# Two output products with their first two blocks interleaved, and the branch sum's high part made by ScalarE

## The chip, the cores and the metric

One core of one Trainium2 chip runs the whole program. The metric is the device time of one execution in microseconds (us), of which the median of several runs is given. The engines are TensorE (PE, with its weight loads as PEld), VectorE (DVE), ScalarE (ACT), GpSimd (POOL) and SyncE (SP), which here issues the loads of weights.

## The reference, cut to what matters

The model is a stack of two blocks of layers over 256 tokens of width 1024: an attention and retention mixer, a short convolution mixer, two layers of product-key experts, and then a second block with a feed-forward layer, a token mixer and another feed-forward layer. Two places matter here, the output products of the convolution mixer and of the token mixer:

```python
def short_conv_mixer(xn, w_in, conv_w, w_out):
    bg, cg, hx = jnp.split(xn @ w_in, 3, axis=-1)
    u = cg * hx
    y = lax.conv_general_dilated(u, ...)
    return (bg * y) @ w_out

def token_mixer(h, ..., w_branch_fox, w_branch_swa, w_out):
    ...
    y = jax.nn.sigmoid(ga) * (o_fox @ w_branch_fox) + jax.nn.sigmoid(gb) * (o_swa @ w_branch_swa)
    return y @ w_out
```

All weights and activations are fp32.

## The kernel before

Activations stand transposed: 128 partitions hold 128 of the 1024 features, so that an activation is K = 8 input parts of 128 x 256 tokens. A weight matrix is cut into output blocks of 128 features; one block is one tile of 128 x 1024, in a ring of four places. SyncE loads it into `ring`. ScalarE rounds it to `ring_hi` (`split_hi`, L508), VectorE makes the rest `ring_lo = ring - ring_hi` (`split_lo`, L514), and TensorE sums three matmuls for each of the eight input parts k (`product3`, L520 to L522): weight high x input high, weight high x input low, weight low x input high. So an output block is 24 matmuls, and its sum stands in one of four PSUM banks (`work`), which VectorE or ScalarE reads and frees.

Every engine runs its own list of instructions in order, with waits on semaphores between them. `split_to(n)` on ScalarE and on VectorE issues the splits of weight tiles up to tile n + 2. The place of a tile in the ring is free for `split_hi` when TensorE has used the tile four before.

The stages around the change are, in order of time:

- `odd()`, the convolution mixer's input products (24 blocks), whose last VectorE steps make the parts `z2_hi`, `z2_lo` of the gated result and count them in `zy_ready`, then `linear("oddout", ...)`, 8 output blocks. For the first block TensorE waits for each input part (`ready(k)`); the later blocks find all parts there. Behind each block `residual` on VectorE adds it to `stream` (L1737) and `split_and_square` on ScalarE begins the next normalisation.
- `attend()`, then `branch()`: for each of 8 output blocks c, TensorE makes two half products of 12 matmuls (`branch_item(c, x)`), from the tile of slot `SLOT0["branch"] + c`. VectorE's `branch()` (L2130 to L2143) splits tile c + 2, multiplies each product with its gate (L2138, twice), adds the two into `mix_y` (L2141), and in `parts` makes the sum's high part (a cast, L1549) and its low part (a subtraction, L1551), which is counted in `branch_ready`. ScalarE in this stage only runs `split_all("branch")`, the splits of tiles c + 2.
- `linear("mixout", ...)`, 8 output blocks whose input parts are these eight sums; with them run `residual` and `split_and_square`, which begins with `load_root()`, an activation whose function (Sqrt) needs another table than the gates' Sigmoid.

Of the kernel before, what the change touches and what calls it, by code (L numbers as in the profile page):

```python
# [16 lines left out]
ALU = mybir.AluOpType  # L17
ACT = mybir.ActivationFunctionType
AX = mybir.AxisListType
F32 = mybir.dt.float32  # L20
# [6 lines left out]
K = D // P  # L27
S = 256
META = 16
TA = META + S  # L30
XS = slice(META, TA)
# [130 lines left out]
W0 = {}  # L162
# [66 lines left out]
SLOTS, SLOT0 = plan_slots()  # L229
# [31 lines left out]
def build(nc, a):  # L261
    with ExitStack() as ctx:
# [3 lines left out]
        def sem(name):  # L266
            return ctx.enter_context(nc.semaphore(name))
# [5 lines left out]
        normed_hi, normed_lo = [x[:, 0:K * TA].rearrange("p (k t) -> p k t", k=K) for x in normed_parts]  # L273
# [38 lines left out]
        work = ctx.enter_context(nc.psum_tensor("work", [P, 4, 512], F32))  # L312
# [14 lines left out]
        def view(group, shape, arena=arena):  # L327

            n = int(np.prod(shape))
            at = used.get(group, 0)  # L330
            used[group] = at + n
            assert used[group] <= ARENA, group
            v = arena[:, at:at + n]
            names = "abcd"[:len(shape)]
            if len(shape) > 1:
                v = v.rearrange(f"p ({' '.join(names)}) -> p {' '.join(names)}",
                                **{x: s for x, s in zip(names[1:], shape[1:])})
            return v
# [21 lines left out]
        z2_hi, z2_lo = [view("odd", [K, S], arena_parts) for _ in range(2)]  # L360
# [61 lines left out]
        mix_y = view("after", [2, S])  # L422
        mix_t = view("after", [2, 2, S])
# [5 lines left out]
        bank_done = [sem(f"bank_done{b}") for b in range(4)]  # L429
        bank_free = [sem(f"bank_free{b}") for b in range(4)]  # L430
        chunk_ready, chunk_used = sem("chunk_ready"), sem("chunk_used")
        hi_ready, lo_ready = sem("hi_ready"), sem("lo_ready")
# [18 lines left out]
        zy_ready = sem("zy_ready")  # L451
# [3 lines left out]
        qksq_ready, qkstd_ready, qk2_ready = sem("qksq_ready"), sem("qkstd_ready"), sem("qk2_ready")  # L455
        forget_in, forget_out, forget_ready = sem("forget_in"), sem("forget_out"), sem("forget_ready")
        table_ready, table_stored, bias_in = sem("table_ready"), sem("table_stored"), sem("bias_in")
        branch_ready = sem("branch_ready")
        first_turned, second_turned, back_done = sem("first_turned"), sem("second_turned"), sem("back_done")
        gains_ready, lead_hi, lead_lo, lead_square = sem("gains_ready"), sem("lead_hi"), sem("lead_lo"), sem("lead_square")  # L460
        sum_ready, sum_done, root_ready, silu_ready = sem("sum_ready"), sem("sum_done"), sem("root_ready"), sem("silu_ready")
# [6 lines left out]
        vec = Tally(sem("vec_step"))  # L468
        own = Tally(sem("act_step"))

        def done(w):
            return bank_done[w % 4], w // 4 + 1

        def freed(w):
            return bank_free[w % 4], w // 4 + 1
# [8 lines left out]
        def wait_bank(pe, w):  # L484

            if w >= 4:
                pe.wait_ge(*freed(w - 4))
# [22 lines left out]
        def split_lo(eng, n, i=0, slots=4):  # L510

            eng.wait_ge(hi_ready, i * slots + (n + 1))
            width = SLOTS[n][2]
            eng.tensor_tensor(ring_lo[:, n % RING, 0:width], ring[:, n % RING, 0:width], ring_hi[:, n % RING, 0:width].bitcast(F32), ALU.subtract).then_inc(lo_ready, 1)  # L514

        def product3(pe, out, n, k, hi, lo, start, stop, **more):

            m = n % RING
            w_hi, w_lo = ring_hi[:, m, k * P:(k + 1) * P], ring_lo[:, m, k * P:(k + 1) * P]
            pe.matmul(out, w_hi, hi, start=start, stop=False, **more)  # L520
            pe.matmul(out, w_hi, lo, start=False, stop=False, **more)  # L521
            return pe.matmul(out, w_lo, hi, start=False, stop=stop, **more)  # L522
# [115 lines left out]
        def _(pe):  # L638
# [117 lines left out]
            def even_out():  # L756
# [4 lines left out]
                for c, k in order:  # L761
# [7 lines left out]
                    if k == K - 1:  # L769
                        mm.then_inc(bank_done[w % 4], 1)  # L770

            def linear(name, hi, lo, width, ready, blocks=K, first=range(K)):

                n = SLOT0[name]
                for c in range(K):
                    w = W0[name] + c
                    wait_bank(pe, w)
                    for y, k in enumerate([*first, *range(K, blocks)] if c == 0 else range(blocks)):
                        if k % K == 0:
                            pe.wait_ge(lo_ready, n + k // K + 1)  # L780
                        if c == 0:
                            pe.wait_ge(*ready(k))
                        mm = product3(pe, work[:, w % 4, 0:width], n + k // K, k % K, hi(k), lo(k), y == 0, y == blocks - 1)
                        if k % K == K - 1 and k < blocks - 1 and blocks > K:
                            mm.then_inc(part_used, 1)
                    mm.then_inc(bank_done[w % 4], 1)
                    n += -(-blocks // K)
# [137 lines left out]
            def odd():  # L925
                project_two(W0["odd"], SLOT0["odd"], XS, lead_lo, 0, then=sum_squares(0))
                for i in range(2, len(ODD_ITEMS)):
                    project(W0["odd"] + i, SLOT0["odd"] + i, XS)

            def feed_forward(x, cols):  # L930
                w, n = W0[f"ffn{x}"], SLOT0[f"ffn{x}"]
                if x == 1:
                    project_two(w, n, cols, lead_lo, K, then=sum_squares(1))
                else:
                    project_raw(w, n, 7, cols)
                for i in range(2, len(FFN_ITEMS)):
                    if x == 1 and i == 24:
                        pe.wait_ge(sum_ready, 1)
                        pe.matmul(acc[:, 1, 0:S], cst("inv_d"), squares4[:, 0, :], start=True, stop=True).then_inc(sum_done, 1)
                    if x == 1:  # L940
                        project(w + i, n + i, cols)
                    else:
                        project(w + i, n + i, slice(0, S), *raw_parts[7])
                linear(f"ffn{x}out", lambda k: ff_hi[:, k, cols], lambda k: ff_lo[:, k, cols], cols.stop - cols.start,
                       lambda k: (ff_ready, FC * (x - 1) + k + 1), FC)
# [120 lines left out]
            def branch():  # L1066
                for c, x in [(1, 0), (0, 1), (1, 1)] + [(c, x) for c in range(2, K) for x in range(2)]:
                    branch_item(c, x)
# [2 lines left out]
            even_out()  # L1071
            peer(0)
            odd()
            linear("oddout", lambda k: z2_hi[:, k, :], lambda k: z2_lo[:, k, :], S, lambda k: (zy_ready, k + 1))
            peer(1)
            feed_forward(1, ALL)
            mix()
            attend()
            branch()
            linear("mixout", lambda k: normed_hi[:, k, XS], lambda k: normed_lo[:, k, XS], S, lambda k: (branch_ready, k + 1))  # L1080
            feed_forward(2, XS)


# [1 line left out]
        def _(act):  # L1085
            ahead = [0]

            def split_to(n):

                while ahead[0] < len(SLOTS) and ahead[0] <= n + AHEAD:  # L1090
                    split_hi(act, ahead[0])
                    ahead[0] += 1
# [15 lines left out]
            def split_all(name, widths=1):  # L1108

                for c in range(K):  # L1110
                    split_to(SLOT0[name] + (c + 1) * widths - 1)
# [378 lines left out]
            def attend():  # L1490
# [17 lines left out]
                for b in range(4):  # L1508
                    for x in range(2):
                        finish_gates(b, x)  # L1510

            act.wait_ge(memset_done, 3)
            first_parts()
            even()
# [7 lines left out]
            norm(6, ALL, first_squares)  # L1522
            mix()
            attend()
            split_all("branch")
            split_and_square("mixout", 7, XS)
            norm(7, XS)
            feed_forward(2, XS)
# [4 lines left out]
        def _(dve):  # L1533
            def step():

                dve.wait_ge(vec.sem, vec.n)
# [3 lines left out]
            def split_to(n):  # L1540

                while ahead[0] < len(SLOTS) and ahead[0] <= n + AHEAD:
                    if not any(ahead[0] in r for r in POOL_SLOTS):
                        split_lo(dve, ahead[0])
                    ahead[0] += 1

            def parts(k, cols, src, ready, hi=normed_hi, lo=normed_lo):

                dve.tensor_copy(hi[:, k, cols], src).then_inc(vec.sem, vec.up())  # L1549
                step()  # L1550
                dve.tensor_tensor(lo[:, k, cols], src, hi[:, k, cols].bitcast(F32), ALU.subtract).then_inc(ready, 1)  # L1551
# [576 lines left out]
                          lambda u: split_to(SLOT0["gates"] + (u - 1) // 2))  # L2128

            def branch():  # L2130
                for c in range(K):
                    w = W0["branch"] + 2 * c
                    b = c % 2
                    split_to(SLOT0["branch"] + c)
                    dve.wait_ge(gate_ready, 2 * (c // 2) + 2)
                    for x in range(2):
                        dve.wait_ge(*done(w + x))
                        dve.tensor_tensor(mix_t[:, b, x, :], work[:, (w + x) % 4, 0:S], gate2[x][:, c, :], ALU.mult).then_inc(bank_free[(w + x) % 4], 1)  # L2138
                    for x in range(2):
                        dve.wait_ge(*freed(w + x))  # L2140
                    dve.tensor_tensor(mix_y[:, b, :], mix_t[:, b, 0, :], mix_t[:, b, 1, :], ALU.add).then_inc(vec.sem, vec.up())  # L2141
                    step()
                    parts(c, XS, mix_y[:, b, :], branch_ready)  # L2143

            for x in normed_parts:
                dve.memset(x[:, K * TA:].bitcast(F32), 0.0)
# [121 lines left out]
```

## Time and profile before

| | |
|---|---|
| median of 3 runs | 2537.78 us (2537.66 to 2538.14) |
| span of the profiled execution, first to last instruction | 2536.0 us |
| what the timed runs have around such a span | about 1.8 us |
| PE busy | 2476.1 us, 98% of the span |
| DVE busy | 1899.6 us, 75% |
| ACT busy | 1251.5 us, 49% |
| `oddout` stage | about 1033.7 to 1056.5 us of the span |
| `branch` and `mixout` stages | about 2293.5 to 2344 us of the span |

The profiled execution is not one of the three timed ones; its span is compared with spans, and the timed runs with timed runs. Times in the rows are us from the start of the span. In rows of a timeline the second number is the length of the instruction, and a bracket at the end is the idle time of the engine before it and what ended it. On VectorE and ScalarE two instructions in a row overlap a little, so the distance between two starts (the pitch) is what one costs on its engine. Matmuls are pipelined too, and only their pitch counts.

### The profile page before, as it was taken

What the parts mean: (1) busy time and instruction counts of PE and PEld (TensorE: products, weight loads), DVE (VectorE), ACT (ScalarE), POOL (GpSimd) and SP (SyncE); (2) the same over time, 40 slices, a digit from 0 to 9 for tenths busy, and PEclk for the clock granted to TensorE, in tenths of its full rate; (3) what the DMA queues carried; (4) which work ended last, traced back from release to release, by engine and by line L of the source; (5) the groups of instructions that cost most, each with busy time, mean ns of one, the idle gap of its engine ahead of it and who ended that gap; (6) DMA issues with size and microseconds to landing.
All of it is one profiled execution on the core that took longest, in us unless ns stands there. A gap on an engine that the chain in (4) does not pass through costs nothing.

```text
span 2536.0 us, 48340 instructions
## 1 busy us (share of the span) xinstructions
PE 2476.1 (98%) x17772; PEld 2278.6 (90%) x17772; DVE 1899.6 (75%) x3683; ACT 1251.5 (49%) x2078; POOL 125.7 (5%) x99
## 2 busy tenths in 40 slices
PE   8999999999999999999999999999999999999999
PEld 8998988999999889999989999998889998778999
DVE  6789997666666887889986666666887757677774
ACT  6754874444444334555864444444344445345443
POOL 0042000000000000051000000000000000000000
PEclk9999999999999999999999999999999999999999
DMA  6445676666655555455776666655545553534554
GB/s 237 145 152 177 193 208 238 211 208 209 211 195 185 188 190 166 160 169 179 206 235 211 212 211 208 209 185 188 187 145 180 175 178 132 112 117 142 183 178 156
DMA packets 192248, 467.22 MB, mean 184 GB/s; under 512 B 81618, under 2 KB 83666, under 8 KB 191200
## 3 DMA queue, kind: packets, MB, share of 16 engines
q1 hardware_dynamic: 118768, 420.52, 50.5%
q0 software_dynamic: 6992, 25.81, 3.7%
q10 hardware_dynamic: 66336, 18.88, 3.1%
q8 instruction: 95, 1.56, 0.2%
q14 instruction: 57, 0.47, 0.1%
HBM read 442.53 MB, written 22.61 MB: 183 GB/s over the span
## 4 chain that ended last, share of the span: by engine, by line
PE 48%; DVE 3%; DMA 1%; ACT 1%; issue 0%; DVEq 0%; ACTq 0%
PE acc L833 14%; PE work L520 9%; PE work L521 9%; PE work L522 9%; PE acc L520 1%; PE acc L521 1%; PE work L847 1%; PE acc L522 1%; DMA ring<-in_gate_in 1%; DVE ring_lo L514 1%; PE work L1062 1%; PE work L1034 0%; PE work L686 0%; PE work L688 0%; PE work L687 0%
## 5 line engine op out<-in xcount | busy, mean ns | idle before, releaser
L514 DVE TENSOR_TENSOR ring_lo<-ring,ring_hi 128x1024 fp32r<-128x1024 f32 (+1 forms) x759 | 923.7, 1220 | 430.0 <-ACT ring_hi L508 428.2
L508 ACT ACTIVATE ring_hi<-ring 128x1024 fp32r<-128x1024 f32 (+1 forms) x799 | 833.6, 1051 | 460.0 <-PE acc L833 369.3
L520 PE MATMUL work<-normed_hi,ring_hi 128*128 128x256 f32 (+1 forms) x2512 | 716.5, 285 | 29.1 <-DVE ring_lo L514 23.7
L521 PE MATMUL work<-normed_lo,ring_hi 128*128 128x256 f32 (+1 forms) x2512 | 710.8, 283 | 0.0
L522 PE MATMUL work<-normed_hi,ring_lo 128*128 128x256 f32 (+1 forms) x2512 | 708.7, 282 | 0.0
L833 PE MATMUL acc<-ring_hi,weighed 128*128 128x512 f32 x2048 | 587.1, 395 | 4.8 <-DVE weighed L1920 4.8
L520 PEld LDWEIGHTS work<-normed_hi,ring_hi 128*128 128x128 f32 x2512 | 475.1, 189 | 42.8 <-DVE ring_lo L514 23.0
L521 PEld LDWEIGHTS work<-normed_lo,ring_hi 128*128 128x128 f32 x2512 | 476.1, 190 | 7.9
L522 PEld LDWEIGHTS work<-normed_hi,ring_lo 128*128 128x128 f32 x2512 | 474.3, 189 | 0.0
L833 PEld LDWEIGHTS acc<-ring_hi,weighed 128*128 128x128 f32 x2048 | 372.9, 188 | 83.6 <-DVE weighed L1920 5.2
L520 PE MATMUL work<-arena_parts,ring_hi 128*128 128x256 f32 (+1 forms) x1184 | 337.6, 285 | 1.7 <-ACT arena L1135 1.1
L522 PE MATMUL work<-arena_parts,ring_lo 128*128 128x256 f32 (+1 forms) x1184 | 334.4, 282 | 0.0
L521 PE MATMUL work<-arena_parts,ring_hi 128*128 128x256 f32 (+1 forms) x1184 | 334.0, 282 | 0.0
L833 PE MATMUL acc<-ring_lo,weighed 128*128 128x512 f32 x1024 | 322.5, 396 | 0.0
L1276 ACT ACTIVATE arena<-work 128x256 f32 (+1 forms) x192 | 73.8, 385 | 348.9 <-PE work L522 348.8
L833 PEld LDWEIGHTS acc<-ring_lo,weighed 128*128 128x128 f32 x1024 | 192.4, 188 | 45.5
L520 PEld LDWEIGHTS work<-arena_parts,ring_hi 128*128 128x128 f32 x1184 | 223.6, 189 | 4.0 <-DVE arena L2138 1.4
L521 PEld LDWEIGHTS work<-arena_parts,ring_hi 128*128 128x128 f32 x1184 | 223.5, 189 | 0.1
L522 PEld LDWEIGHTS work<-arena_parts,ring_lo 128*128 128x128 f32 x1184 | 223.5, 189 | 0.0
L1914 DVE TENSOR_TENSOR product<-arena 128x256 f32 (+1 forms) x256 | 157.0, 613 | 2.5 <-ACT arena L1290 2.5
L520 PE MATMUL acc<-normed_hi,ring_hi 128*128 128x256 f32 x512 | 157.0, 307 | 0.0
L521 PE MATMUL acc<-normed_lo,ring_hi 128*128 128x256 f32 x512 | 143.9, 281 | 0.0
(283 smaller groups left out, 2511.5 us busy)
## 6 DMA issues: line engine op xcount, KB each, us to landing
ring<-in_u SPq DMA_DIRECT2D x256, 512.0 KB, 3.4
ring<-in_v SPq DMA_DIRECT2D x256, 512.0 KB, 3.3
ring<-in_ffn_in SPq DMA_DIRECT2D x88, 512.0 KB, 3.3
ring<-in_query SPq DMA_DIRECT2D x32, 512.0 KB, 3.4
ficients_of_later_chunks<-gate_b ACTq DMA_DIRECT2D x32, 512.0 KB, 4.6
arena<-ficients_of_later_chunks POOLq DMA_DIRECT2D x32, 512.0 KB, 4.4
ring<-in_ffn_out SPq DMA_DIRECT2D x32, 512.0 KB, 3.9
ring<-in_even_in SPq DMA_DIRECT2D x28, 512.0 KB, 4.1
```

The source lines that it names most:

```text
L508: act.activation(ring_hi[:, n % RING, 0:width], ring[:, n % RING, 0:width], ACT.Copy).then_inc(hi_ready, 1)
L514: eng.tensor_tensor(ring_lo[:, n % RING, 0:width], ring[:, n % RING, 0:width], ring_hi[:, n % RING, 0:width].bitcast(F32), ALU.subtract).t ...
L520: pe.matmul(out, w_hi, hi, start=start, stop=False, **more)
L521: pe.matmul(out, w_hi, lo, start=False, stop=False, **more)
L522: return pe.matmul(out, w_lo, hi, start=False, stop=stop, **more)
L833: mm = pe.matmul(acc[:, 2 * half + t, :], tokens, rows[:, m, half * 512:(half + 1) * 512], start=(e == 0 and x == 0), stop=(e == CHUNKS - ...
L847: mm = pe.matmul(work[:, w % 4, t * P:(t + 1) * P], hot_second[b][:, t // 2, :, t % 2], hot_gated[b][:, x, t // 2, :, t % 2], start=(x == ...
L1062: mm = pe.matmul(work[half, w % 4, t * P:S], v, prob2[0:rows, u % 2, b, t:NT, :].rearrange("p t q -> p (t q)"), start=(b == 0), stop=(b == ...
L1276: act.activation(into, work[:, w % 4, 0:S], ACT.Gelu).then_inc(bank_free[w % 4], 1)
L1914: dve.tensor_tensor(product[:, e % 2, :], hid, co, ALU.mult).then_inc(coef_read, 1)
```

## The change

It has three parts. The output products `oddout` and `mixout` no longer run block by block from the start: the first two blocks, c = 0 and 1, are interleaved, first input parts 0 to 6 of block 0, then parts 0 to 6 of block 1, then part 7 of each; blocks 2 to 7 follow as before. In the branch stage the high part of each sum is made by ScalarE instead of VectorE. And VectorE makes the low part of block c - 1 behind the sum of block c, instead of behind its own sum.

```diff
+            def linear_two_first(name, hi, lo, ready):
+                n, w0 = SLOT0[name], W0[name]
+                order = [(c, k) for c in range(2) for k in range(K - 1)] + [(c, K - 1) for c in range(2)] + [(c, k) for c in range(2, K) for k in range(K)]
+                for c, k in order:
+                    w = w0 + c
+                    if k == 0:
+                        wait_bank(pe, w)
+                        pe.wait_ge(lo_ready, n + c + 1)
+                    if c == 0:
+                        pe.wait_ge(*ready(k))
+                    mm = product3(pe, work[:, w % 4, 0:S], n + c, k, hi(k), lo(k), k == 0, k == K - 1)
+                    if k == K - 1:
+                        mm.then_inc(bank_done[w % 4], 1)
...
-            linear("oddout", lambda k: z2_hi[:, k, :], lambda k: z2_lo[:, k, :], S, lambda k: (zy_ready, k + 1))
+            linear_two_first("oddout", lambda k: z2_hi[:, k, :], lambda k: z2_lo[:, k, :], lambda k: (zy_ready, k + 1))
...
-            linear("mixout", lambda k: normed_hi[:, k, XS], lambda k: normed_lo[:, k, XS], S, lambda k: (branch_ready, k + 1))
+            linear_two_first("mixout", lambda k: normed_hi[:, k, XS], lambda k: normed_lo[:, k, XS], lambda k: (branch_ready, k + 1))
...
# ScalarE
+            def branch():
+                for c in range(K):
+                    split_to(SLOT0["branch"] + c)
+                    act.wait_ge(branch_sum, c + 1)
+                    act.activation(normed_hi[:, c, XS], mix_y[:, c % 2, :], ACT.Copy).then_inc(branch_hi, 1)
...
-            split_all("branch")
+            branch()
...
# VectorE
             def branch():
+                def low_part(c):
+                    dve.wait_ge(branch_hi, c + 1)
+                    dve.tensor_tensor(normed_lo[:, c, XS], mix_y[:, c % 2, :], normed_hi[:, c, XS].bitcast(F32), ALU.subtract).then_inc(branch_ready, 1)
+
                 for c in range(K):
...
-                    dve.tensor_tensor(mix_y[:, b, :], mix_t[:, b, 0, :], mix_t[:, b, 1, :], ALU.add).then_inc(vec.sem, vec.up())
-                    step()
-                    parts(c, XS, mix_y[:, b, :], branch_ready)
+                    if c >= 2:
+                        dve.wait_ge(branch_ready, c - 1)
+                    dve.tensor_tensor(mix_y[:, b, :], mix_t[:, b, 0, :], mix_t[:, b, 1, :], ALU.add).then_inc(branch_sum, 1)
+                    if c:
+                        low_part(c - 1)
+                low_part(K - 1)
```

## Rows read from the trace of the kernel before

**Rows 1.** The page's head and its busy times.
```profile
span 2536.0 us, 48340 instructions
...
PE 2476.1 (98%) x17772; PEld 2278.6 (90%) x17772; DVE 1899.6 (75%) x3683; ACT 1251.5 (49%) x2078; POOL 125.7 (5%) x99
```

**Rows 2.** Windows: stretch, length, busy PE, PEld, DVE, ACT, POOL, granted clock, DMA share, GB/s.
```profile
1034.00:1057.00 23.00, 23.00 (x197) 23.00 (x196) 18.33 (x31) 12.46 (x21) 0.00 (x0) 1.00 0.56 185
2298.00:2319.00 21.00, 20.80 (x163) 19.58 (x164) 19.79 (x41) 8.90 (x10) 0.00 (x0) 1.00 0.53 175
```

**Rows 3.** Waits from 2294 to 2330 us: total us, times, longest.
```profile
ACT ring_hi L508 <- PE work L522: 10.8, 6, 2.1
...
PE work L520 <- DVE normed_lo L1551: 2.0, 1, 2.0
```

**Rows 4.** Timeline of VectorE, the branch stage's begin and its last block.
```profile
2296.23 1.23 DVE L514 TENSOR_TENSOR ring_lo<-ring,ring_hi 128x1024 fp32r<-128x1024 f32 x1 [1.76 <-ACT ring_hi L508]
2297.49 0.42 DVE L2138 TENSOR_TENSOR arena<-work,desk 128x256 f32<-128x256 f32 x1
...
2318.20 1.22 DVE L514 TENSOR_TENSOR ring_lo<-ring,ring_hi 128x1024 fp32r<-128x1024 f32 x1
2319.33 0.42 DVE L2138 TENSOR_TENSOR arena<-work,desk 128x256 f32<-128x256 f32 x1
2319.67 0.42 DVE L2138 TENSOR_TENSOR arena<-work,gate_b 128x256 f32<-128x256 f32 x1
2320.19 0.43 DVE L2141 TENSOR_TENSOR arena<-arena 128x256 f32<-128x256 f32 x1
2320.65 0.29 DVE L1549 CAST normed_hi<-arena 128x256 fp32r<-128x256 f32 x1
2320.97 0.43 DVE L1551 TENSOR_TENSOR normed_lo<-arena,normed_hi 128x256 fp32r<-128x256 f32 x1
2321.32 1.22 DVE L514 TENSOR_TENSOR ring_lo<-ring,ring_hi 128x1024 fp32r<-128x1024 f32 x1
```

**Rows 5.** Timeline of TensorE, the first matmul of the output product's input part 7.
```profile
2321.45 0.39 PE L520 MATMUL work<-normed_hi,ring_hi 128*128 128x256 f32 x1 [2.02 <-DVE normed_lo L1551]
```

**Rows 6.** Timeline of ScalarE in the branch stage.
```profile
2295.12 3.92 ACT L508 ACTIVATE ring_hi<-ring 128x1024 fp32r<-128x1024 f32 x4
...
2311.53 1.28 ACT L1115 ACT_TABLE_LOAD   x1
2312.83 0.20 ACT L1115 ACTIVATE small<-small 128x1 f32<-128x1 f32 x1
```

**Rows 7.** Timeline of VectorE and ScalarE in a normalisation.
```profile
1065.56 0.48 DVE L1569 SCALAR_TENSOR_TENSOR gate_b<-stream,const,rstd 128x256 f32<-128x256 f32 x1
...
1066.08 0.42 ACT L1105 ACTIVATE normed_hi<-gate_b 128x256 fp32r<-128x256 f32 x1 [1.72 <-DVE gate_b L1569]
1066.40 0.37 ACT L1135 ACTIVATE arena<-work 128x256 f32<-128x256 f32 x1
```

**Rows 8.** Timeline of VectorE and TensorE at the last input part of `oddout`'s first block.
```profile
1035.66 0.43 DVE L1551 TENSOR_TENSOR arena_parts<-arena,arena_parts 128x256 fp32r<-128x256 f32 x1
...
1036.24 0.29 PE L520 MATMUL work<-arena_parts,ring_hi 128*128 128x256 f32 x1
```

**Rows 9.** TensorE's long gaps (timeline), its pitch at the lower clock, and a window of it.
```profile
1296.84 0.73 PE L833 MATMUL acc<-ring_hi,weighed 128*128 128x512 f32 x2 [2.46 <-DVE weighed L1920]
...
2111.04 0.36 PE L686 MATMUL work<-ring_hi,normed_hi 128*128 128x256 f32 x1 [2.62 <-DVE ring_lo L514]
...
2160.22 0.38 PE L984 MATMUL work<-const,arena 8*128 8x8 f32 x2 [2.52 <-DVE arena L2104]
...
2290.33 0.41 PE L522 MATMUL work<-arena_parts,ring_lo 128*128 128x256 f32 x1
2290.54 0.41 PE L520 MATMUL work<-arena_parts,ring_hi 128*128 128x256 f32 x1
...
2112.10:2115.30 3.20, 3.20 (x18) 3.20 (x17) 3.17 (x3) 0.00 (x0) 0.00 (x0) 0.50 0.82 292
```

More of the change, by code:

```diff
@@ L457, in build @@
         table_ready, table_stored, bias_in = sem("table_ready"), sem("table_stored"), sem("bias_in")
-        branch_ready = sem("branch_ready")
+        branch_ready, branch_sum, branch_hi = sem("branch_ready"), sem("branch_sum"), sem("branch_hi")
         first_turned, second_turned, back_done = sem("first_turned"), sem("second_turned"), sem("back_done")
```

## The prediction

> **What bounds the kernel now.** I read the page first, then windows over the two stages that the change touches, then the waits there, and at last the timelines, engine by engine. The page says that TensorE is busy for 98% of the span [rows 1]. So work taken off another engine is worth only what TensorE waits for it.
>
> In `oddout` it waits for nothing: 23.00 us busy of 23.00, 197 matmuls, 0.117 us each [rows 2]. The last input part of the first block is the place that an interleaving could help. Its low part starts on VectorE at 1035.66 and takes 0.43, so it is there at 1036.09; TensorE comes to it at 1036.24 with no idle time before it [rows 8]. There is nothing to win.
>
> The branch stage is another case. VectorE is busy 19.79 of 21.00 us there [rows 2] and sets the pace. One block on it, from split to split, takes 3.12 us (2318.20 to 2321.32), by pitches: split 1.13, first product 0.34, second product and the wait for it 0.52, sum 0.46, cast 0.32, low part 0.35 [rows 4]. TensorE's 24 matmuls need only 24 x 0.117 = 2.8 us. ScalarE is idle for more than half of the stage, and its splits are early: the first four run in one piece from 2295.12, up to three blocks before VectorE asks for them [rows 6]; later ones wait for TensorE to free a place of the ring [rows 3], still ahead of VectorE. At the end TensorE has done parts 0 to 6 of the first output block and waits 2.02 us for the last sum's low part [rows 3, 5].
>
> **The change part by part: `oddout`.** Same 192 matmuls in another order. Gain: none, as above. Loss: block 0 is done some 2.5 us later (21 matmuls of block 1 stand before its last three), so VectorE's first residual starts later, and the split of tile 3, which stands behind it in VectorE's list, too. TensorE wants tile 3 only after three blocks, 8.5 us after the stage's start at about 1033.75, so at 1042.3; VectorE then has it at about 1041. The cover is 1.3 us; were it gone, each us late would be a us lost. Sum: 0, with at most 0.2 either way.
>
> **The branch stage.** What VectorE loses is the cast and the two waits of a chain: sum to cast 0.46 and cast to low part 0.32 become a plain pitch of about 0.34 (as between the two products). Its own work falls from 3.12 to 1.13 + 0.34 + 0.52 + 0.34 + 0.34 = 2.67 us a block, below TensorE's 2.8.
>
> What is added is a wait on ScalarE, and what matters is what is queued behind it. ScalarE's list is now: split tile c + 2, wait for sum c, copy, split tile c + 3. VectorE's is: low half of tile c + 2, products, sum c, low part c - 1, low half of tile c + 3. So tile c + 3, which ScalarE used to split blocks ahead, now stands behind the copy of sum c, and VectorE's next block begins with that tile. The two engines take turns. One round, from VectorE's sum to its next sum:
>
> - sum, until ScalarE starts the copy: 0.43 long [rows 4] plus 0.04 for the signal (1065.56 + 0.48 = 1066.04, ScalarE starts at 1066.08 [rows 7]): 0.465
> - copy of 128 x 256 from memory to memory, high part out: pitch 0.32, the same form in a normalisation, 1066.08 to 1066.40 [rows 7]
> - split of the tile until VectorE starts its half: 1.09. Four splits take 3.92, three pitches of 0.96 and one whole length of 1.05 [rows 6]; the signal adds 0.04
> - VectorE's split 1.13, products 0.34 and 0.52 [rows 4]: 1.99
>
> Together 3.865 us in place of 3.12, 0.745 more. The low part (0.34) and a wait of some 1.1 for ScalarE lie inside the round. The first tile of the stage is split by both engines as before, so there are 7 such rounds: 7 x 0.745 = 5.2. An instruction behind a wait starts a little later than behind a busy engine; for 7 times 0.02 I add 0.1. The ScalarE copy is not in this stage's trace, so both bounds: not less than the cast's 0.29 on VectorE [rows 4], 0.2 less in all; not more than its full length 0.42 instead of its pitch, and VectorE's split followed by its product after 1.26 as at 2296.23 instead of 1.13 [rows 4], together 7 x (0.10 + 0.13) = 1.6 more. I take the pitches, because seven of eight rounds before ran by them.
>
> TensorE has slack in this: 2.8 us of matmuls in 3.87, 73%.
>
> **The output product.** The wait for the last sum is now met otherwise. Low part 6 comes behind sum 7, so it, not part 7, is what TensorE waits for. Before, low part 7 starts 0.78 after sum 7; now low part 6 starts 0.34 after it, 0.44 earlier. After the wait TensorE has 30 matmuls up to the end of block 1 instead of 27 (part 6 and 7 of block 0, all of block 1): 3 x 0.117 = 0.35 more. Low part 7 is ready 0.9 after sum 7 and has 24 matmuls to hide behind. So the interleaving wins nothing that isn't lost again: -0.44 + 0.35 = -0.1. Sum so far: 5.2 + 0.1 - 0.1 = 5.2; in absolute times sum 7 starts at 2320.19 + 5.3 = 2325.5, TensorE resumes 0.34 + 0.48 later (2320.97 to 2321.45 [rows 4, 5]) at 2326.3 and ends block 1 at about 2329.9.
>
> Next late is the table load. It ran at 2311.53 in ScalarE's idle time; now it stands behind copy 7 and in front of the split of tile 2 of `mixout`: copy 2325.97, load 2326.4, 1.30 and then 0.2 [rows 6], split at 2327.9, VectorE's half at 2329.0, its end 1.22 later at 2330.2. TensorE would want it at 2329.9: 0.3 lost. The sum is then 5.5 with this wait. The Trainium skill ("ScalarE: Activation LUTs", "What ACT_TABLE_LOAD costs") puts a switch of tables at about 2.7 us, its drain included, where the row has 1.30 to the next instruction; by that figure this wait would be 1.7, and the sum 6.9. After this tile VectorE has more than 0.5 us of slack a block and the stage is TensorE's again.
>
> **The clock.** TensorE's idle time in front of part 6: with VectorE's first product of block 6 at about 2320.8, it starts the output product at 2321.3, runs 18 matmuls to 2323.5 and resumes at 2326.3, so 2.8 us, with another idle us just before these 18. Before the change the longest gaps were 2.62 and 2.52, and behind both the granted clock fell to 0.50, the level of 1.2 GHz; 2.46 (and 2.0 in this very place) left it at 1.00, 2.4 GHz [rows 5, 9]. The slow stretch behind the gap of 2.62 is at least 3.2 us long, and the pitch in one is 0.21 instead of 0.117 [rows 9]: 3.2 x (1 - 0.117 / 0.21) = 1.4 us lost. It would hide the 0.3 of the table load, since TensorE then wants the tile later. I take the fall as likelier than not, for the gap is longer than any in the trace: 5.2 + 1.4 = 6.6.
>
> **Rivals.** A measurement of this kernel tells 0.2%, 5.1 us, from no change.
>
> - The chain, with the clock held: 5.2 + 0.3 = 5.5, so 2543.3. For it: the gap of 2.46 passed. Against it: 2.52 and 2.62 did not.
> - The table load costs twice its row, because the engine must be empty around it: 0.3 + 1.3, 6.8 with the clock held, 2544.6. Against it: 1.30 from its start to the next start [rows 6]. The Trainium skill's figure for a switch, above, would be this case.
> - As meant, faster: the splits stay ahead and the stage is TensorE's. 7 x (3.12 - 2.82) = 2.1 less, and the wait of 2.0 is hidden behind block 1: -4.1, 2533.7. It decides as soon as ScalarE's split of tile c + 3 is issued before its wait for sum c. Against it stands the order of the list, which `split_to` with its two tiles ahead fixes; for it only ScalarE's idle share.
> - It does little: a round much shorter than its rows, or lost time taken back in `mixout`, between 0 and +4.5. Against it: `mixout` is bound by TensorE, with nothing to take back.
>
> **How the numbers follow.** The chain with the fall 0.48, the chain with the clock held 0.31, the dear table load 0.06, as meant 0.05, little 0.10. The likeliest is 2537.78 + 6.6 = 2544.4 (against the profiled span of 2536.0, which lies 1.8 below the median: 2542.6). Low end: the chain with the copy at its lower bound and no wait for a tile is 5.0, and a part of "little" should be inside: 2542.0. High end: 6.6 + 1.6 = 8.2, so 2546.0. Slower by over 0.2%, that is above 2542.86: nearly all of the fall and of the dear load, three quarters of the held clock: 0.78. Faster 0.05. The rest, 0.17, is within 0.2%.
>
> **What the profile after would show.** In the branch stage L514 on VectorE waits for ScalarE's `ring_hi` seven times, some 1.1 us each; starts of L514 lie 3.87 apart; no cast writes `normed_hi`; eight copies of 0.42 on ScalarE, each followed at once by a split. TensorE has gaps of about a us per block, then one of 2.8 before part 6, and a granted clock of 0.50 for some 3 us behind it. `oddout` keeps 0.117 a matmul without a gap. The prediction is wrong if VectorE's rounds are near 2.8 (the splits are ahead after all), if a gap opens in `oddout`, or if the clock stays at 1.00 and TensorE waits for no tile behind the table load.

## The result and the profile after

The changed kernel takes 2541.97 us in the median of 14 runs (2540.5 to 2546.0), the kernel before 2537.72 us (14 runs, 2536.14 to 2538.88): a ratio of 1.0018, 95% interval 1.0012 to 1.0025. So it is slower: the interval is 3.0 to 6.3 us, and the two medians differ by 4.25 us. (Here and below, the ratio of two medians can differ from the ratio given by up to 0.0004; it lies inside the interval each time.) The forecast range of 2542.0 to 2546.0 was 4.2 to 8.2 us above the 2537.78 us that it started from. The result stands at its lower end, 0.03 us outside it as an absolute time and 0.03 us inside it as a difference, and well under the likeliest value of 6.6 us. The profiled execution has a span of 2539.8 us, 3.8 us more than before.

In the waits from 2294 to 2334 us, ScalarE and VectorE now stand first, each waiting for the other (columns as in [rows 3]; L1531 is ScalarE's copy of the sum, L2168 the sum, L2163 a product with a gate, L2154 the low part):

```profile
ACT normed_hi L1531 <- DVE arena L2168: 19.9, 8, 2.6
DVE ring_lo L514 <- ACT ring_hi L508: 12.5, 9, 2.4
...
PE work L520 <- DVE arena L2163: 5.3, 7, 0.8
...
PE work L520 <- DVE normed_lo L2154: 2.6, 1, 2.6
```

Before, VectorE waited for nothing between its blocks, and TensorE's one long wait was 2.02 us [rows 3, 5]. The timeline of VectorE, its last two rounds (sum is L2168, low part L2154, tile split L514), answers to [rows 4]:

```profile
2316.48 0.43 DVE L2168 TENSOR_TENSOR arena<-arena 128x256 f32<-128x256 f32 x1
2316.82 0.42 DVE L2154 TENSOR_TENSOR normed_lo<-arena,normed_hi 128x256 fp32r<-128x256 f32 x1
2318.34 1.22 DVE L514 TENSOR_TENSOR ring_lo<-ring,ring_hi 128x1024 fp32r<-128x1024 f32 x1 [1.10 <-ACT ring_hi L508]
2319.49 0.42 DVE L2163 TENSOR_TENSOR arena<-work,desk 128x256 f32<-128x256 f32 x1
2319.82 0.41 DVE L2163 TENSOR_TENSOR arena<-work,gate_b 128x256 f32<-128x256 f32 x1
2320.32 0.43 DVE L2168 TENSOR_TENSOR arena<-arena 128x256 f32<-128x256 f32 x1
2320.67 0.42 DVE L2154 TENSOR_TENSOR normed_lo<-arena,normed_hi 128x256 fp32r<-128x256 f32 x1
2322.18 1.23 DVE L514 TENSOR_TENSOR ring_lo<-ring,ring_hi 128x1024 fp32r<-128x1024 f32 x1 [1.10 <-ACT ring_hi L508]
2323.32 0.42 DVE L2163 TENSOR_TENSOR arena<-work,desk 128x256 f32<-128x256 f32 x1
...
2324.16 0.42 DVE L2168 TENSOR_TENSOR arena<-arena 128x256 f32<-128x256 f32 x1
```

And the timeline of ScalarE over the last of these, which answers to [rows 6] (copy L1531, tile split L508, table load L1130):

```profile
2320.78 0.42 ACT L1531 ACTIVATE normed_hi<-arena 128x256 fp32r<-128x256 f32 x1 [2.47 <-DVE arena L2168]
2321.11 1.04 ACT L508 ACTIVATE ring_hi<-ring 128x1024 fp32r<-128x1024 f32 x1
2324.62 0.42 ACT L1531 ACTIVATE normed_hi<-arena 128x256 fp32r<-128x256 f32 x1 [2.47 <-DVE arena L2168]
2325.06 1.28 ACT L1130 ACT_TABLE_LOAD   x1
2326.35 0.20 ACT L1130 ACTIVATE small<-small 128x1 f32<-128x1 f32 x1
2326.46 1.99 ACT L508 ACTIVATE ring_hi<-ring 128x1024 fp32r<-128x1024 f32 x2
```

The two read together are the chain: sum at 2320.32, copy at 2320.78 (0.46 later), tile split at 2321.11 (0.33), VectorE's half at 2322.18 (1.07), next sum at 2324.16 (1.98): 3.84 us, with 1.10 of it VectorE's wait and 2.47 ScalarE's. In the first of the seven rounds VectorE waits 1.43 us, since no low part stands in it yet; in the other six it waits 1.10. Behind the last copy stands the table load, where before it ran at 2311.53 in idle time.

TensorE's gap in front of part 6, its step to the third output block (tile 2), VectorE's wait for that tile, and the windows of `oddout` and of the gap (columns as in [rows 2]):

```profile
2324.98 0.39 PE L520 MATMUL work<-normed_hi,ring_hi 128*128 128x256 f32 x1 [2.62 <-DVE normed_lo L2154]
...
2328.51 0.28 PE L522 MATMUL work<-normed_hi,ring_lo 128*128 128x256 f32 x1
2328.91 0.36 PE L520 MATMUL work<-normed_hi,ring_hi 128*128 128x256 f32 x1
...
2327.53 1.23 DVE L514 TENSOR_TENSOR ring_lo<-ring,ring_hi 128x1024 fp32r<-128x1024 f32 x1 [2.04 <-ACT ring_hi L508]
```

```profile
1034.00:1057.00 23.00, 23.00 (x197) 23.00 (x196) 18.38 (x32) 12.18 (x22) 0.00 (x0) 1.00 0.57 186
2322.40:2324.90 2.50, 0.00 (x0) 0.00 (x0) 2.41 (x5) 0.28 (x1) 0.00 (x0) 1.00 0.22 46
2325.00:2330.00 5.00, 4.88 (x39) 4.71 (x40) 2.89 (x4) 4.29 (x8) 0.00 (x0) 1.00 0.29 99
```

VectorE's half of tile 2 ends at 2328.76, and TensorE's first matmul with it follows at 2328.91. `oddout` is as full as before. In this execution the clock stayed at 1.00 behind the gap.

**A measure that is sharper than the whole time.** I take as the stage the time from VectorE's first tile split of the branch stage to ScalarE's reading (L1117, L1102 before) of the next normalisation's sum. Before it is 2296.23 to 2344.97, 48.74 us; after it is 2295.15 to 2349.09, 53.94 us: +5.20. Before the stage the profiled execution of the changed kernel is 1.08 us early; the last section shows in which stretches, in which both kernels do the same work. 5.20 - 1.08 is 4.1, behind the stage another 0.3 us is won, and the spans differ by 3.8.

### The profile page after: what moved, and what is told of

The parts are those of the page before. It is cut to its first block and busy times, and to the rows that moved or that the text cites. A ratio compares the mean times of both kernels' runs of the same rounds, so it can differ in the third digit from the quotient of the medians.

```text
span 2539.8 us, 48340 instructions
## 1 busy us (share of the span) xinstructions
PE 2475.8 (97%) x17772; PEld 2278.7 (90%) x17772; DVE 1897.2 (75%) x3675; ACT 1254.4 (49%) x2086; POOL 125.7 (5%) x99
## 5 line engine op out<-in xcount | busy, mean ns | idle before, releaser
L514 DVE TENSOR_TENSOR ring_lo<-ring,ring_hi 128x1024 fp32r<-128x1024 f32 (+1 forms) x759 | 921.8, 1218 | 438.1 <-ACT ring_hi L508 436.3
L508 ACT ACTIVATE ring_hi<-ring 128x1024 fp32r<-128x1024 f32 (+1 forms) x799 | 833.6, 1050 | 448.9 <-PE acc L848 370.9
```

Of the source, the lines that this page charges most:

```text
L508: act.activation(ring_hi[:, n % RING, 0:width], ring[:, n % RING, 0:width], ACT.Copy).then_inc(hi_ready, 1)
```

## The experiments

Theory: ScalarE's tile split stands behind its wait for the sum, and this turn-taking is nearly the whole cost. Rivals: the interleaving delays what comes behind block 0; handing a sum to another engine costs in itself; and, on the size, the clock behind TensorE's gap. The first four kernels were timed with 28 runs of the kernel before on the same chip (median 2538.16 us), the fifth with 15 (2538.34 us); the others have one execution each, the profiled one (copy made twice with the split ahead 2532.92 us, low part at once 2534.78, table load early 2545.89 and 2545.11, changed kernel again 2542.84, 2542.08 and 2541.17).

**Interleaving alone.** `linear_two_first` for both products, the rest as before:

```diff
-            linear("oddout", ...)
+            linear_two_first("oddout", ...)
...
-            linear("mixout", ...)
+            linear_two_first("mixout", ...)
```

> Both output products interleaved, everything else as before (VectorE makes both parts of the branch sum, ScalarE splits tiles without a wait on a sum). The stage is measured from VectorE's first tile split of the branch stage to ScalarE's reading of the last normalisation's sum: 48.7 us before, 53.9 us after the change. If the added time is the turn-taking of ScalarE and VectorE, then this kernel has none of it and also loses the wait of 2.0 us in front of part 7, which block 1 covers: stage 46.7 us, time 2 us under the kernel before. If the interleaving is what costs (block 0 done later, residual and tiles late), the stage is near 53.9 us. oddout should be the same length in both.

Measured: stage 46.81 us, 1.93 less than before; time 2534.96 us, ratio 0.9991 (0.9982 to 1.0). TensorE has no gap over 0.25 us from the second block of the branch stage to the end of the output product, and VectorE's blocks are 3.12 us apart. The interleaving is no cost; here it takes back the whole wait. `oddout`'s first matmul to the next normalisation's is 24.97 us here, 24.98 before: nothing won or lost there.

**The high part on ScalarE and the delayed low part alone**, both products block by block (against the changed kernel):

```diff
-            linear_two_first("oddout", ...)
-            linear_two_first("mixout", ...)
+            linear("oddout", ...)
+            linear("mixout", ...)
```

> The high part on ScalarE and the low part one block later, but both output products block by block as before. If the turn-taking costs everything: rounds of 3.84 us on VectorE, and without the interleaving the wait for the last low part comes 0.5 us after that for low part 6 but 3 matmuls fewer stand between, so the stage is 53.9 to 54.2 us: the interleaving is worth nothing beside the delayed low parts. If the interleaving costs: stage near 48.7 us.

Measured: stage 54.08 us, time 2541.83 us, ratio 1.0018 (1.0009 to 1.0027). The whole loss is in this part. The interleaving, worth 1.93 us beside VectorE's own cast, is worth 0.14 us behind the chain: what TensorE waits for is low part 6, and block 1 can hide only what comes after it.

**ScalarE's split one tile further ahead**, one edit in the changed kernel:

```diff
                 for c in range(K):
-                    split_to(SLOT0["branch"] + c)
+                    split_to(SLOT0["branch"] + c + 1)
                     act.wait_ge(branch_sum, c + 1)
```

> The changed kernel with one edit: ScalarE splits tile c + 3 before it waits for sum c, not behind the copy. If the order in ScalarE's list is the cause, VectorE no longer waits for the tile: its rounds fall from 3.84 to TensorE's 2.82 us or a little above, TensorE's wait in front of part 6 shrinks, the stage is about 44.6 us, and the time is some 4 us under the kernel before (9 us under the changed one in the stage). If the handing over of the sum to another engine itself is the cost, whatever stands behind it, the stage stays near 53.9 us.

Measured: stage 45.06 us (44.6 expected), 8.88 under the changed kernel and 3.68 under the kernel before; time 2533.25 us, ratio 0.9984 (0.9975 to 0.9993). A round of VectorE's timeline and ScalarE's over the same stretch:

```profile
2303.02 0.43 DVE L2168 TENSOR_TENSOR arena<-arena 128x256 f32<-128x256 f32 x1
2303.36 0.42 DVE L2154 TENSOR_TENSOR normed_lo<-arena,normed_hi 128x256 fp32r<-128x256 f32 x1
2303.69 1.22 DVE L514 TENSOR_TENSOR ring_lo<-ring,ring_hi 128x1024 fp32r<-128x1024 f32 x1
...
2305.67 0.42 DVE L2168 TENSOR_TENSOR arena<-arena 128x256 f32<-128x256 f32 x1
...
2303.47 0.42 ACT L1531 ACTIVATE normed_hi<-arena 128x256 fp32r<-128x256 f32 x1 [1.28 <-DVE arena L2168]
2303.80 1.05 ACT L508 ACTIVATE ring_hi<-ring 128x1024 fp32r<-128x1024 f32 x1
```

VectorE splits at 2303.69 a tile that ScalarE had finished at 2302.20; the one that ScalarE splits at 2303.80 is the next. VectorE's round is 2.65 us without a wait. The same copy, the same hand-over, the same interleaving: the order of two instructions in one list is the 8.9 us. In that figure is the wait for tile 2, since its split now stands in front of the last copy and the table load. Against the interleaving alone the stage is 1.75 us shorter (46.81 to 45.06) and the median time 1.71: that is what the hand-over gains once nothing waits behind it.

**The copy made twice**, in the changed kernel and in the version with the split ahead:

```diff
                     act.wait_ge(branch_sum, c + 1)
+                    act.activation(product[:, c % 2, :], mix_y[:, c % 2, :], ACT.Copy)
                     act.activation(normed_hi[:, c, XS], mix_y[:, c % 2, :], ACT.Copy).then_inc(branch_hi, 1)
```

> The changed kernel, with a second copy of each sum by ScalarE (into memory that nobody reads) in front of the one that counts. It changes nothing that is computed. If ScalarE's copy is in the round, each of 7 rounds grows by the pitch of 0.32 us to 4.16 us, and the table load behind the last copy is 0.32 us later: stage 53.9 + 2.2 to 2.6 = 56.1 to 56.5 us. If ScalarE has slack (it is idle 60% of the stage), the stage stays at 53.9 us. TensorE's gap in front of part 6 grows to about 2.9 us, so here the lower clock should follow it more often than in the changed kernel; with it 1.4 us more.

> The version with the split one tile ahead and a second, useless copy of each sum in front of the one that counts. There ScalarE's copy should lie outside VectorE's and TensorE's rounds: round 2.65 us as without it, stage 45.1 to 45.4 us (the last low part comes 0.3 us later, behind block 1's matmuls). In the changed kernel the same copy cost 0.31 us a round. If ScalarE's copy is on the path here too, rounds of 2.96 us and a stage near 47 us.

Measured: in the changed kernel rounds of 4.15 us instead of 3.84 and a stage of 57.38 us, 3.44 more (time 2545.52 us in 6 runs, 3.55 more; ratio to the kernel before 1.0031, 1.0019 to 1.0043); in the other, rounds of 2.65 us and a stage of 45.06 us, no change. The 3.44 are more than the first expectation's 2.6 at the clock of before: 7 x 0.31 = 2.2 from the rounds, and the clock fell behind a gap of 2.94 us, to 0.50 for some 3.4 us (about 1.5 us), which hides the wait of 0.3 for the third tile.

**The split ahead, without the interleaving in `mixout`.**

> The version with ScalarE's split one tile ahead (stage 45.06 us), but with mixout block by block again. It prices the interleaving in the version in which the chain is gone. There VectorE's rounds are 2.65 us and TensorE is the bound of the branch stage, so the sums are done early and little is left to wait for in front of parts 6 and 7. If the interleaving's 1.9 us (seen with VectorE's own cast) is a gain of its own, the stage goes to about 46.9 us; if its worth was only the wait that the slow VectorE left, the stage is 45.1 to 45.8 us.

Measured: stage 45.28 us, time 2533.35 us, ratio 0.9978 (0.9969 to 0.9987). Only 0.22 us of stage is left for the interleaving: with VectorE's round shorter than TensorE's 2.8 us there is hardly a wait that it could cover. The two best kernels are not told apart by time.

**The low part directly behind its own sum**, with the split ahead:

```diff
-                    if c >= 2:
-                        dve.wait_ge(branch_ready, c - 1)
                     dve.tensor_tensor(mix_y[:, b, :], ...).then_inc(branch_sum, 1)
-                    if c:
-                        low_part(c - 1)
-                low_part(K - 1)
+                    low_part(c)
```

> The version with the split one tile ahead, but each low part directly behind its own sum, as before the change, and not one block later. VectorE then waits for ScalarE's copy: signal, copy at full length and signal back, 0.93 us from sum to low part instead of 0.34. Rounds 1.13 + 0.34 + 0.52 + 0.93 + 0.34 = 3.26 us instead of 2.65, longer even than the 3.12 us with VectorE's own cast. Against the interleaved kernel with that cast (stage 46.8 us) 7 x 0.14 more: stage 47.8 us. If the delay of the low part by a block is not needed, rounds stay at 2.65 to 2.82 us and the stage at 45.1 us.

Measured: rounds of 3.23 us, stage 47.65 us. VectorE's low part starts 0.91 us after its sum, 0.48 us of it idle:

```profile
2300.03 0.42 DVE L2168 TENSOR_TENSOR arena<-arena 128x256 f32<-128x256 f32 x1
2300.94 0.43 DVE L2154 TENSOR_TENSOR normed_lo<-arena,normed_hi 128x256 fp32r<-128x256 f32 x1 [0.48 <-ACT normed_hi L1531]
```

So the hand-over does cost when it is waited for at once, more than VectorE's own cast; the change's delay by a block is what makes it free. Of the change, the delay is worth 2.6 us of stage, and the split ahead is what it lacked.

**The table load early**, in the changed kernel, profiled twice:

```diff
             def branch():                    # ScalarE
+                load_root()
                 for c in range(K):
                     split_to(SLOT0["branch"] + c)
```

with the call at the begin of `split_and_square("mixout", ...)` left out.

> The changed kernel, but the activation that brings in the Sqrt table is issued at the begin of ScalarE's branch list and not behind its last copy. The table load then runs while ScalarE waits for sum 0. By my sum the load costs 0.2 to 0.3 us of TensorE's time at the third output block: stage 53.94 down to 53.6 or 53.7 us, VectorE's wait for that tile down from 2.04 us to about 0.6 us. If the load costs its whole 1.28 us or more: stage 52.6 us or less. If the gates' table has to be loaded again for the copies: more than 53.9 us.

> The changed kernel with the Sqrt table brought in at the begin of ScalarE's branch list, once more, since in its first execution the clock fell behind the gap and covered the wait for the third tile. If the clock holds here: stage 53.94 - 0.3 = 53.65 us, and TensorE's step from the second to the third output block is 0.12 us and not 0.40. If it falls: 55.2 or 56.4 us, as for the changed kernel.

Measured: stages of 55.24 and 55.11 us. In both the clock fell behind the gap of 2.63 us, for one stretch of 3.4 us, so what the load cost in the changed kernel can't be read off them; it stands in the rows above (a step of 0.40 us to the third output block instead of 0.12). VectorE's wait for that tile did fall, from 2.04 to 0.53 us. But I had put the load in the wrong place. On ScalarE:

```profile
2294.99 0.61 ACT L1504 ACTIVATE gate_b<-acc 128x512 f32<-128x512 f32 x1
2295.61 1.28 ACT L1130 ACT_TABLE_LOAD   x1
2296.91 0.20 ACT L1130 ACTIVATE small<-small 128x1 f32<-128x1 f32 x1
2297.02 1.04 ACT L508 ACTIVATE ring_hi<-ring 128x1024 fp32r<-128x1024 f32 x1
```

The first tile's split stands behind it, VectorE waits for that tile (3.85 us instead of 2.41), and the stage begins 1.5 us late, which my measure of the stage does not count. The load wants the idle time behind the first split, not in front of it.

**The changed kernel, three more profiles.**

> The changed kernel itself once more, to see how often the granted clock falls behind TensorE's gap of 2.63 us in front of part 6. Forecast theory: it falls in more than half of the executions, then 1.3 us are added to the stage (53.94 to about 55.2 us). Rival: a gap of this length in this place never brings it down, stage 53.94 us again. Elsewhere in the span (behind the gap of 2.46 us at 1297 us, and around 2157 and 2287 us) the slow stretches should come and go from one execution to the next by themselves.

> The changed kernel once more. In one profiled execution the clock held behind the gap of 2.63 us in front of part 6 (stage 53.94 us), in another it fell in it and stayed low for 6.6 us (stage 56.35 us). Expected is one of three lengths: 53.9 us (held), about 55.2 us (one slow stretch of 3.4 us), about 56.4 us (two).

> The changed kernel once more, for the same count: 53.9, 55.2 or 56.4 us of stage.

Measured: 56.35, 54.08 and 53.94 us. With the first profile, the clock held in three of four. Where it fell, TensorE and the windows show it:

```profile
2323.76 0.58 PE L520 MATMUL work<-normed_hi,ring_hi 128*128 128x256 f32 x1 [2.63 <-DVE normed_lo L2154]
2324.14 0.41 PE L521 MATMUL work<-normed_lo,ring_hi 128*128 128x256 f32 x1
2324.35 0.41 PE L522 MATMUL work<-normed_hi,ring_lo 128*128 128x256 f32 x1
```

```profile
2321.20:2323.20 2.00, 0.00 (x0) 0.00 (x0) 1.91 (x4) 0.00 (x0) 0.00 (x0) 0.99 0.00 0
2323.60:2329.80 6.20, 6.04 (x28) 6.04 (x29) 1.75 (x3) 3.60 (x5) 0.00 (x0) 0.50 0.40 149
```

The clock is at its lower level when TensorE resumes, the pitch is 0.21 us, and the stage is 2.4 us longer than where it held. The gap is 2.62 to 2.64 us in all four. It is 2.63 in the two kernels with the early load too, where the clock fell both times, and 2.65 with the high part alone, where it held: behind the same gap it fell in three of seven profiles.

## Why the prediction was right, and what was off

- **The turn-taking of ScalarE and VectorE.** Right, and shown: taken away by one edit in ScalarE's list it is gone, and a doubled copy lengthens each round by its pitch. The forecast round of 3.865 us measured 3.84 (the first 3.85), VectorE's forecast wait of 1.1 us is 1.10 in six rounds and 1.43 in the first. By the first split, sum 7 was forecast 5.3 us later than before and is 5.05 later (29.01 after the first split, 23.96 before): the 0.02 a round for instructions behind a wait was not there, and the signals were 0.01 to 0.02 shorter.
- **The output product.** Right: TensorE waits for low part 6, 0.34 + 0.47 us behind sum 7, and has 30 matmuls from there. The interleaving is worth 0.14 us behind the chain and 1.93 us without it, both measured alone.
- **The table load.** Forecast 0.3 us; the step to the third block is 0.28 us longer than a matmul's pitch, and the load to the next start is 1.29 us. The Trainium skill's figure for a switch of tables ("ScalarE: Activation LUTs", "What ACT_TABLE_LOAD costs") is about 2.7 us with its drain, and the estimate from it was 1.7. Here the load starts 0.02 us behind the last copy's end, and the rows decide against it.
- **The clock.** This is the term that was mis-sized: 1.4 us for a fall was part of the likeliest sum, at 0.48 against 0.31 for no fall. The reason given for it was a wrong comparison. The 2.8 us was reckoned from the pitch of the last matmul (0.117), and so counted the gap did measure 2.8 (2322.07 + 0.117 to 2324.98). The 2.62, 2.52 and 2.46 of [rows 9] are idle times from the matmul's end, 0.28 behind its start; in that measure the gap is 2.62 to 2.64, like the longest before. Nor did [rows 9] sort the falls by length: the pitch of 0.21 at 2290.33 stands behind no idle time over 1.45 us. Behind this gap the clock held in three of four profiles of the changed kernel, and in four of seven with the other kernels that have the same gap, so neither chance is refuted; the error is that the price of a fall went whole into the likeliest sum. Where the clock fell in the changed kernel it cost 2.4 us, not 1.4: the slow stretch was 6.8 us long, its 6.2 us of matmuls at a pitch of 0.21 instead of 0.117 cost 2.7, and the 0.3 of the table load was hidden. The trace of before already had a stretch of that length, behind its gap of 2.52 (last section). Without the fall the forecast was +5.5 for the stage, and the stage grew by 5.20: 5.05 in the rounds, 0.28 at the tile, -0.1 in the output product.
- **`oddout`.** Right: 24.96 us from its first matmul to the next normalisation's, 24.98 before.
- **The rival "as meant"** said -4.1 us once the split is issued before the wait. With exactly that edit the stage is 3.68 us shorter than before. In the changed kernel as it is, the order of the list stood against it, as forecast.
- **The sum.** The medians differ by 4.25 us, while the stage grew by 5.20, and by 7.6 in an execution with the fall. So about 1 us came back outside the stage, which no term of the forecast held; with a likeliest value 2.4 us too high, it is partly luck that the result still met the lower end of the range. The profiles have the same: the four of the changed kernel reach the stage 0.8 to 2.3 us earlier than the one of the kernel before, and their spans (2539.4 to 2541.0) are 3.4 to 5.0 us longer than its 2536.0. With one profile of the kernel before it stays open whether this is the change's doing; the last section shows where it arises.

## What to carry to other kernels

When an instruction with a new wait is put into an engine's list, look at what stands behind it there and who waits for that, not at the engine's idle share: ScalarE was idle more than half of the stage and the 0.33 us copy cost 5 us, because a tile split stood behind its wait. Issue the work that doesn't depend on the wait first; with that one step the same change is a gain. Here the cast that was handed to another engine paid only where its result was taken up a block later (stage 45.06 us against 47.65), and the interleaving paid only what was still waited for: 1.93 us beside the slow VectorE, 0.22 once the stage in front of it was fast. When a forecast gap is compared with idle times of a trace, both must be counted from the same end.

## What the runs showed of the hardware

The same work outside the change differs between executions by steps of 1.5 and 2.5 us, with the granted clock. From the first matmul behind the wait near 1297 us to the experts' end (L905 before, L920 after) the kernel before takes 585.67 us and the changed one 587.21, in spans in which both do the same. The windows show where:

```profile
1297.00:1303.00 6.00, 6.00 (x26) 4.83 (x27) 5.86 (x10) 1.90 (x3) 0.00 (x0) 1.00 0.88 254
```

is the kernel before, behind its gap of 2.46 us [rows 9], and

```profile
1297.00:1303.00 6.00, 6.00 (x20) 4.75 (x20) 4.98 (x9) 1.52 (x2) 0.00 (x0) 0.73 0.93 252
```

the changed one, behind the same gap. Of the 14 profiles of this study seven have 585.7 us there and seven 587.1 to 587.2.

From the matmul near 2160 us to VectorE's first split of the branch stage it is 136.0 us in two profiles (the kernel before among them) and 133.5 in the ten others without an early table load. The windows of the kernel before and of the changed one:

```profile
2161.00:2167.00 6.00, 6.00 (x27) 5.90 (x27) 4.52 (x5) 1.16 (x2) 1.10 (x1) 0.53 0.62 93
...
2157.40:2160.20 2.80, 2.80 (x14) 2.77 (x13) 2.77 (x4) 0.06 (x1) 0.00 (x0) 0.50 0.48 146
```

In the kernel before the slow stretch lies behind the gap of 2.52 us, and the 2.5 us are lost. In the changed one it lies in front of the same gap: TensorE comes to it later, waits only 0.95 us instead of 2.52, and nothing is lost, because the matmul behind it waits for VectorE.

So the profile of the kernel before paid nothing at the first place and 2.5 us at the second, and the changed one paid 1.5 at the first and nothing at the second; that, with 0.13 us earlier in the span, is its 1.08 us head start. It can't be put down to chance without more: of the eight profiles of kernels in which ScalarE's split stands behind its wait seven have the slow stretch near 1297 us, of the six others none, although that place lies a millisecond in front of the stage. No run here shows why.

Counted over all profiles, the idle time of a gap does not tell whether the clock falls in it or just behind it: 2.38 us near 372 us, in 4 of 14; 2.46 near 1297, in 7 of 14; 2.52 near 2160, in 2 of the 9 that come to it at full clock; 2.56 to 2.63 near 2112, in 14 of 14; 2.62 to 2.65 in front of part 6, in 3 of 7; 2.94 there, in the one profile that has it. One profile can't say what such a gap costs: a difference below 3 us in this kernel is read from a stage in both profiles, or from many runs.
